# Routing each token tile inside the last quarter of the output projection, in a hybrid RG-LRU, SSD and mixture-of-experts layer

## What is computed

```python
x = x + concatenate([y_lru, y_ssd]) @ w_out          # output projection
h = rms_norm(x, norm_ffn)
c_logits = h @ w_coarse + b_coarse                   # 4 groups
g_idx, g_w = argmax(c_logits), softmax(c_logits)[g_idx]
f_logits = (h @ w_fine + b_fine)[g_idx]              # 8 experts of that group
f_val, f_idx = top_k(f_logits, 2)
expert = g_idx * 8 + f_idx                           # 2 assignments for each token
# assignments are put in blocks of 128 rows, each block of one expert
for each block: yb = (silu(xb @ w_gate[e]) * (xb @ w_up[e])) @ w_down[e]
out = x + sum over the token's two rows of yb * weight
```

## Time and profile before

| what | value |
|---|---|
| median of 3 runs | 1502.64 us (1501.02 to 1502.64) |
| the profiled execution, its own time | 1498.86 us |
| its span in the profile | 1497.0 us |
| PE busy | 92% of the span |
| DVE, ACT, POOL busy | 65%, 53%, 37% |
| the chain that ended last, by engine | PE 82%, DVE 8%, POOL 3%, ACT 2%, DMA 2% |
| last quarter of the projection | 722.76 to 782.74 us |
| from there to the first product of the first expert block | 67.29 us, to 850.03 us |
| mean granted clock of PE | 0.956 |

### The profile page before, as it was taken

How to read it: one execution, slowest core, us unless ns; L and a number is a source line. 1 busy time by engine, 2 the same in 40 slices (tenths; PEclk the granted TensorE clock), 3 DMA queues, 4 the chain that set the end, 5 groups by cost and what they waited for, 6 DMA issues and landing times.

```text
span 1497.0 us, 19671 instructions
## 1 busy us (share of the span) xinstructions
PE 1372.8 (92%) x6510; PEld 1131.8 (76%) x6510; DVE 977.4 (65%) x918; ACT 786.8 (53%) x845; POOL 554.7 (37%) x485
## 2 busy tenths in 40 slices
PE   7999999999999999899992599999999999999950
PEld 5888888888888787688782478888888888888740
DVE  5433433575555758800326388999999998998857
ACT  5342214355434546200132178888888888888844
POOL 2444444766555666948003112211221112112112
PEclk9999999999999999999995699999999999999985
DMA  4112112233322244514214189999999999999756
GB/s 168 55 48 78 49 49 87 75 107 109 102 88 80 73 131 155 176 52 163 108 57 154 54 298 396 383 379 378 376 376 379 383 391 382 395 383 390 269 205 267
DMA packets 99540, 308.68 MB, mean 206 GB/s; under 512 B 15648, under 2 KB 17568, under 8 KB 99360
## 3 DMA queue, kind: packets, MB, share of 16 engines
q1 hardware_dynamic: 89840, 291.17, 53.5%
q0 software_dynamic: 9648, 16.80, 3.0%
HBM read 293.62 MB, written 32.64 MB: 218 GB/s over the span
## 4 chain that ended last, share of the span: by engine, by line
PE 82%; DVE 8%; POOL 3%; ACT 2%; DMA 2%; issue 1%; SPq 0%; DVEq 0%; ACTq 0%; POOLq 0%
PE ps L843 34%; PE ps L558 28%; PE ps L719 9%; PE ps L832 2%; DVE X L1594 2%; PE ps L665 2%; PE ps L674 2%; POOL M L1663 1%; PE ps L795 1%; DMA ring_dn<-in_moe 1%; PE ps L863 1%; POOL GH L1638 1%; PE ps L652 1%; POOL GL L1640 1%; PE ps L645 1%
## 5 line engine op out<-in xcount | busy, mean ns | idle before, releaser
L1638 POOL TENSOR_TENSOR GH<-raw,ones 128x512 fp32r<-128x512 f32 x106 | 132.9, 1254 | 293.6 <-PE ps L558 253.8
L558 PE MATMUL ps<-XH,GH 128*128 128x512 f32 x656 | 206.7, 394 | 0.4 <-DVE T L1334 0.4
L558 PE MATMUL ps<-XL,GH 128*128 128x512 f32 x656 | 203.7, 390 | 0.0
L558 PE MATMUL ps<-XH,GL 128*128 128x512 f32 x656 | 203.4, 389 | 0.0
L1640 POOL TENSOR_TENSOR GL<-raw,GH 128x512 fp32r<-128x512 f32 x106 | 156.6, 1477 | 8.3
L1535 DVE TENSOR_TENSOR split_c<-ring_gu,split_c 128x1024 fp32r<-128x1024 f32 x127 | 149.7, 1219 | 1.1 <-ACT split_c L1083 1.1
L558 PEld LDWEIGHTS ps<-XH,GL 128*128 128x128 f32 x656 | 123.1, 188 | 26.0
L558 PEld LDWEIGHTS ps<-XL,GH 128*128 128x128 f32 x656 | 123.2, 188 | 25.8
L558 PEld LDWEIGHTS ps<-XH,GH 128*128 128x128 f32 x656 | 121.3, 188 | 26.7 <-issue 1.7
L843 PE MATMUL ps<-split_c,XTH 128*128 128x512 f32 x520 | 139.8, 391 | 0.0
L1083 ACT ACTIVATE split_c<-ring_gu 128x1024 fp32r<-128x1024 f32 x130 | 130.1, 1049 | 1.6 <-PE ps L843 1.0
(11 more groups left out here) (285 smaller groups left out, 2872.8 us busy)
## 6 DMA issues: line engine op xcount, KB each, us to landing
ring_gu<-in_moe SPq DMA_DIRECT2D x264, 512.0 KB, 5.8
ring_dn<-in_moe SPq DMA_DIRECT2D x132, 512.0 KB, 6.7
raw<-in_win SPq DMA_DIRECT2D x82, 256.0 KB, 2.7
T<-acs_d SPq DMA_DIRECT2D x16, 512.0 KB, 5.3
raw<-in_wout SPq DMA_DIRECT2D x32, 256.0 KB, 2.7
T<-in_x SPq DMA_DIRECT2D x8, 512.0 KB, 7.3
X<-in_x SPq DMA_DIRECT2D x8, 512.0 KB, 4.4
h_d<-M SPq DMA_DIRECT2D x8, 512.0 KB, 2.6
```

Source lines behind the costliest of these rows:

```text
L558: mm = pe.matmul(ps[:, bank + h, :], wp[:, w, col], x[:, kk, h * 512:(h + 1) * 512], start=(kk == 0 and n == 0), stop=(kk == KT - 1 and n ...
L1638: link(pool, pool.tensor_tensor(hi, raw[:, r, :], one.to_broadcast([P, GR]), ALU.mult), g_hi, at + 1)
```

## The change

**Loop.** The last quarter goes in four parts for each tile (`last_quarter`) with the routing of earlier tiles between them. In iteration t, PE turns the second half of `X2` of tile t - 1 and the first half of tile t (`turn_x2`, the rows as they are, not normalized), ranks tile t - 2 (`ranks`), makes the logits of t - 1 (`logits`) and adds tile t - 3 to the table (`table`). DVE does `first_choice(t - 1)`, the addition to `X2`, `second_choice(t - 1)`, reciprocal and `H2`, and `placed(t - 2)`. The router's weights are multiplied by `norm_ffn` once (PE turns `nrow` in front of the loop), and the logits by the reciprocal root, when DVE takes them from PSUM.

**Tables.** The loop makes the table of the first 32 blocks alone, into `tab_i[:, :, 0:NE]`, and `tab_ready` follows it. The table of the overflow blocks is made inside the first block: `overflow_rows` on DVE behind `rows_lo(0)`, 16 products on PE behind `turn_rows(1, 1)`, `overflow_table` on DVE behind `hidden_lo(0)`, with `ov_ready` for SP and POOL.

**Around it.** The one-hot operands of the table lie in the last slot of `ring_gu`, so that chunk is loaded after `tab_ready`, and SP's first reloads stand behind the same wait. POOL clears `XBS` right after the last product, splits chunks 0 to 2 ahead of the wait for `tab_ready`, and 3 to 5 behind the first two gathers. ACT's square goes to `raw`. Some semaphores are merged (`hrow_in` and `tri_in` to `more_in`, `clamped`, `g_hi`, `dev2`).

```diff
 # SP
-            for j in range(KT):
+            for j in range(KT - 1):
                 sp.dma_start(ring[j], a["moe"][j]).then_inc(wch_in[j], 16)
...
             for j in range(KT, CH):
                 sp.dma_start(ring[j], a["moe"][j]).then_inc(wch_in[j], 16)
+            sp.wait_ge(tab_ready, 1)
+            sp.dma_start(ring[KT - 1], a["moe"][KT - 1]).then_inc(wch_in[KT - 1], 16)
 # PE
+            def turn_x2(t, half):
+                if half == 0:
+                    wait(pe, x2t0, t)
+                else:
+                    pe.wait_ge(x2_done, t + 1)
+                    wait(pe, x2t1, t)
+                for k in range(4):
...
+            def ranks(t):
+                pe.wait_ge(rk_in, t + 1)
+                if t < TT - 1:
+                    wait(pe, ab_in, t)
+                else:
+                    pe.wait_ge(x2_done, TT)
+                out = ps[:, rank_bank(t), 0:NE]
+                mm = pe.matmul(out, above, r_sum[t % 2], start=True, stop=(t == 0))
+                if t > 0:
+                    mm = pe.matmul(out, ones[:, :], r_pre[t % 2], start=False, stop=True)
+                mm.then_inc(rk_mm, 1)
+            def table(t):
+                pe.wait_ge(ab_in, t + 1)
+                for k in range(2):
+                    mm = pe.matmul(ps[:, 7, 0:2 * NE], r_A[t % 2][:, k, :], ...
+                mm.then_inc(tab_used, 1)
...
+            for t in range(TT):
                 if t >= 2:
-                    turn_h2(t - 2)
-                if t < TT:
-                    last_half(t, 1)
+                    pe.wait_ge(x2_done, t - 1)
+                last_quarter(t, 0)
+                if t >= 1:
+                    turn_x2(t - 1, 1)
+                turn_x2(t, 0)
                 if t >= 2:
-                    route(t - 2)
-            turn_h2(TT - 1)
-            route(TT - 1)
+                    ranks(t - 2)
+                last_quarter(t, 1)
+                if t >= 1:
+                    if t == 1:
+                        pe.wait_ge(wr_ready, 1)
+                    logits(t - 1, 0)
+                    logits(t - 1, 1)
+                last_quarter(t, 2)
+                if t >= 3:
+                    table(t - 3)
+                last_quarter(t, 3)
+            logits(TT - 1, 0)
+            turn_x2(TT - 1, 1)
+            logits(TT - 1, 1)
+            ranks(TT - 2)
+            table(TT - 3)
+            table(TT - 2)
+            ranks(TT - 1)
...
+            table(TT - 1)
...
             turn_rows(1, 1)
+            overflow_table()
             turn_hidden(0)
 # DVE
+            def placed(t):
+                dve.wait_ge(rk_mm, t + 1)
+                st.link(dve.tensor_tensor(
+                    r_hit, r_M[:, t, :, :], ps[:, rank_bank(t), 0:NE].unsqueeze(1).to_broadcast(
+                        [P, 2, NE]), ALU.mult))
+                reduce(r_rk[:, t, :], r_hit, ALU.add)
+                link(dve, dve.tensor_tensor(
+                    r_A[t % 2], iota.unsqueeze(1).to_broadcast([P, 2, P]),
+                    r_rk[:, t, :].unsqueeze(2).to_broadcast([P, 2, P]), ALU.is_equal),
+                    ab_in, t + 1)
...
             for t in range(TT):
+                if t >= 1:
+                    first_choice(t - 1)
                 x2 = X2[:, t, 512:D]
                 dve.wait_ge(last_mm, t + 1)
                 link(dve, dve.scalar_tensor_tensor(x2, ..., ALU.mult, ALU.add), x2_done, t + 1)
-                dve.wait_ge(dev2, t + 1)
+                if t >= 1:
+                    second_choice(t - 1)
+                dve.wait_ge(dev_ready, TT + t + 1)
...
                 if t >= 2:
-                    logits(t - 2)
+                    placed(t - 2)
+            first_choice(TT - 1)
+            second_choice(TT - 1)
+            placed(TT - 2)
+            placed(TT - 1)
+            dve.wait_ge(tab_used, TT)
+            link(dve, dve.tensor_scalar(tab_i[:, :, 0:NE], ...), tab_ready, 1)
 # POOL
             pool.wait_ge(last_mm, TT)
-            for j in range(HL):
...
+            st.link(pool.memset(XBS[0], 0.0))
+            st.link(pool.memset(XBS[1], 0.0))
+            for j in range(HL // 2):
+                to_lo(j)
             pool.wait_ge(tab_ready, 1)
...
-            for b in range(4):
+            for b in range(2):
+                gather(b, b, 0)
+            for j in range(HL // 2, HL):
+                to_lo(j)
+            for b in range(2, 4):
                 gather(b, b % 2, b - 1)
```

More of the change, by code:

```diff
@@ L316, in build, with tiles_of, tile @@
[L316 to L322, removed]
+        lg_mm, lg_done = sems("lg_mm", "lg_done")
+        def tiles_of(region):
+            at = [0]
+            def tile(*dims):
+                n = int(np.prod(dims))
+                t = region[:, at[0]:at[0] + n]
+                at[0] += n
+                assert at[0] <= region.shape[1]
+                if len(dims) == 2:
+                    return t.rearrange("p (a b) -> p a b", b=dims[1])
+                if len(dims) == 3:
+                    return t.rearrange("p (a b c) -> p a b c", b=dims[1], c=dims[2])
+                return t
+            return tile
@@ L790, in route @@
[L790 to L797, removed]
+                if q == 3:
+                    mm.then_inc(last_mm, 1)
+            def turn_x2(t, half):
[5 more added lines that the diff above has]
+                for k in range(4):
+                    col = (4 * half + k) * P
+                    mm = pe.transpose(ps[:, 4 + half, k * P:(k + 1) * P],
+                                      X2[:, t, col:col + P], ident[:, :])
+                mm.then_inc(tr1_mm if half else tr0_mm, 1)
@@ new lines, in logits @@
+            def logits(t, half):
+                if half == 0:
+                    pe.wait_ge(x2t0, t + 1)
+                    wait(pe, lg_done, t - 1)
+                else:
+                    pe.wait_ge(x2t1, t + 1)
+                for k in range(4 * half, 4 * half + 4):
+                    mm = pe.matmul(ps[:, 3 if t % 2 else 6, 0:NR], H2T[:, k, :], wr[:, k, :],
+                                   start=(k == 0), stop=(k == KT - 1))
+                if half == 1:
+                    mm.then_inc(lg_mm, 1)
@@ L1471, in per_choice @@
-            def per_choice(table, out):
-                for k in range(2):
-                    st.link(dve.tensor_tensor(r_tmp, r_M[k], table, ALU.mult))
-                    st.link(dve.tensor_reduce(out[:, k * TT:(k + 1) * TT], r_tmp, AX_X, ALU.add))
+                    placed(t - 2)
[4 more added lines that the diff above has]
+            dve.wait_ge(tab_used, TT)
+            link(dve, dve.tensor_scalar(
+                tab_i[:, :, 0:NE], ps[:, 7, 0:2 * NE].rearrange("p (q e) -> p q e", q=2), 8192.0,
+                None, ALU.add), tab_ready, 1)
```

352 lines of the change are left out of this document (183 added, 169 removed).

## The result

The changed kernel takes **1526.18 us** (median of 4 runs, 1524.18 to 1528.96), the kernel before 1501.83 in the same comparison: a ratio of 1.0165, 95% interval 1.0153 to 1.0177. It is slower, as forecast, but by 24 us instead of 4, and outside the range of 1495 to 1512. The profiled execution has a span of 1522.4 us, and 1524.18 as its own time, 25.3 over that of before.

A forecast was written before the change was run, and what follows sets the result against it. PE was busy 92%, idle mainly in a 67.29 us serial chain between projection and first expert block. Loop +35.1, tail -33.1, first blocks +2.0 gave +4.0 us, forecast 1506.5 us, range 1495 to 1512.

The forecast's parts named there:

- The loop: PE's own work: Loop over the last quarter: added transposes, logits, ranks and table products on PE lengthen it by 10.7 us.
- The loop: the wait that the pipeline does not hide: At the ranks PE idles for DVE's round, 3.5 us in iterations 3 to 7 and 0.35 in iteration 2: 17.9 us.
- The loop: the clock: Half clock behind the five 3.5 us idle times in the loop: 1.3 us each, bounds 0 and 2.0, 6.5 us.
- The third rival: In the loop the clock stays low for longer, half of the logits too: 5 x 1.5 us more, 1514; chance 0.1.
- The tail: From the projection's last product (E) to the first expert product: 34.2 us in place of 67.29, saving 33.1.
- the lock: Tail before tab_ready: POOL's first three splits each hold one DVE instruction of the chain, 5.4 us.
- The clears of the row buffers: Tail, beside DVE's chain: could hold DVE from 0 to 1.9 us; taken as 0.
- the gather: Tail behind tab_ready: meets 2 MB of SP's loads and takes 0 to 2.5 us more, taken as 2.4.
- The first blocks: First expert blocks: the overflow tables moved into them cost 2 us (0 to 3.5).
- the late split: First blocks: ten added DVE instructions, 3.1 us, delay a split that had 2.0 us in hand: 1.1 us.
- That the splits do not hold DVE up: Rival on the tail: POOL's splits leave DVE and the gather unhindered, tail 25.2 us, kernel 1497.6; chance 0.2.
- That PE doesn't wait at the ranks: Rival on the loop: it hides the routing, growth falls from 35.1 to 10.7 us, kernel 1482; chance 0.05.

The follow-up runs named there:

- The version without waits: The ranks of tile t - 2 moved behind the third quarter of the projection, against the changed kernel: 1480.75 us.
- the two versions that kept one or three: Unused products filling the waits ahead of the ranks in iterations 4 to 7, or only 4 and 6, against the changed kernel: 1508.99 and 1517.66 us.

## Why the prediction was right or wrong

**The loop: PE's own work**, 10.7 forecast: right. The version without waits takes 61.95 us from first to last addition, for 52.61 before, and the turned norm row makes the first iteration longer by 1.3 (8.74 to 7.47): 10.6.

**The loop: the wait that the pipeline does not hide**, 3.5 us five times and 0.35 once, 17.9: right, 19.1 measured. DVE's round was read link by link from instructions that the trace of before had, and each long wait came out 0.2 to 0.3 us over the forecast.

**The loop: the clock** is the step that failed: 5 x 1.3 = 6.5 forecast, 23.4 measured. I priced a 3.7 us wait by the stretches at 0.50 behind 1.79 and 2.12 us of idle time, took the 2.0 us loss of one of them as the upper bound, and went below it. That stretch was 3.4 us long and had wide products behind it. In the loop four of the five stretches were 10.2 or 13.7 us long, most of it on work, with the logits in it, and 3.7 us waits cost 1.9 to 6.1 us each, 4.9 when alone. The bound fails at its own length too: 2.2 us waits in the loop cost 0.2 to 5.0, where 1.9 us waits cost nothing four times of five. An upper bound from one wait in another place, shorter and with other work behind it, was none. Which of these sets how long the half clock lasts stays open; the runs show the sizes, and shorter stretches in the version where the logits came later. The third rival named the right mechanism, but its 5 x 1.5 more was bounded by the same rows, so that the range ended at 1512. By the Trainium skill ("TensorE: Matmul & The Clock Gate", HAM oscillation) the penalty comes back with each wait of a loop; the trace agrees with that, at 4.9 us for each wait in the two versions that kept one or three.

**The tail**, 34.2 forecast, 36.2 measured. Up to `tab_ready` it was right: E + 20.7 forecast, and POOL takes the table up at E + 21.3; three instructions held, the lock 4.9 us by experiment for 5.4. The clears of the row buffers held nothing: the 32-element product at 836.34, within the first of them, took 0.19 us. Behind it two terms were too small, and since they lie side by side only the larger counted: the gather took 4.0 us longer than before (2.4 forecast), and one DVE instruction was held through all three splits, 7.6 us, where I had each split catch one instruction and let it go; DVE was free 2.0 us later than forecast. That the gather's delay comes from the reloads is shown (8.3 to 4.5 us with the reloads late).

**The first blocks**, 2.0 forecast, 2.1 measured. The forecast wait for the late split, 1.1 us, is there with 0.96 (PE before 897.71 us). Most of the rest is in the 16 products of the overflow tables: they were forecast to cost nothing in place of the 2.40 us of idle time, and from the first expert product to the one behind them it takes 17.8 us for 17.1.

**The rivals.** That the splits do not hold DVE up was wrong (4.9 us). That PE doesn't wait at the ranks was wrong for this order, and what it would have given, 1482, is what moving the ranks gave: 1480.75. Of what the forecast missed, the clock's term is 16.9 us, the waits' 1.2 and the tail's 2.0: 1506.5 + 16.9 + 1.2 + 2.0 is 1526.6, for 1526.18. That it comes so near is in part luck, since the forecast starts from a median of 1502.64 that was 1501.83 in the comparison, and 1.7 us of the growth were not followed.

## What to carry to other kernels

Do not take the price of a PE wait from the row of a shorter one, or of one with other work behind it: two waits of 2.19 us cost 0.2 and 5.0 us here. Where a loop makes PE wait a few us in each round, put the waiting instruction behind work that is ready, before counting what the moved work saves. Work from a serial tail fits into a loop only as far as the round of the other engine (here DVE's 5.7 us from the last product to the signal) ends before PE asks for it. And look for the second limit beside the first: an edit that measures as nothing can be half of one worth 3.7 us.

## What the runs showed of the hardware

- Behind a 3.7 us wait of PE the granted clock was 0.50 (1.2 GHz) while PE was busy without a break, up to 763.4 us behind a wait that ended at 753.95; behind 1.9 us waits it stayed at 1.00 (2.4 GHz) four times of five. One and the same wait of 2.12 us ahead of the loop was followed by 0.50 in ten traces and by 1.00 in four. Eighty products that do nothing for the result made a kernel 23 us faster.
- A 16-element DVE instruction was held for 7.61 us beside three POOL splits that followed each other closely, and for 8.66 us from the third to the last of six; each got through only when the whole series was over. In the chain ahead of `tab_ready` an instruction was let go at the end of each split, and the next one caught by the next. What makes the difference no run shows.
- An indirect gather of 128 rows took 8.2 us to PE's use of it beside the reloads of the weight ring, and 4.5 with these held back.
